# Four moved waits in a hybrid decoder layer: GLU weights, last transposes, Strassen operands, last GELU

## The reference

```
z = rmsnorm(h);  u,q,k,v,g,gate_a,gate_b = split(z @ W_in)
y = s5_scan(u) + D*u;  y = gelu(y);  y_a = y * sigmoid(y @ w_glu + b_glu)
y_b = retention(q,k,v) * silu(g)
h = h + (sigmoid(gate_a)*(y_a @ P_A) + sigmoid(gate_b)*(y_b @ P_B)) @ W_out
z = rmsnorm(h)
out = rmsnorm(h + relu(z @ W_up)^2 @ W_down)
```

## Time and profile before

| | |
|---|---|
| median of 3 runs | 1547.04 us (1545.83 to 1547.98) |
| the profiled execution | 1545.83 us, of which the span is 1544.0 us |
| granted TensorE clock | 0.995 of full speed over the span |
| busy share of the span | PE 98%, PE weight load 82%, DVE 61%, POOL 28%, ACT 20% |
| chain that ended last | PE 89%, DVE 7%, ACT 2% |
| one f32 matmul of 512 columns | starts 0.227 us after the one before it |

### The profile page before, as it was taken

The page is one execution under the profiler, slowest core; times in us unless marked ns, Lnnn a source line. Parts: engine busy times, 40 slices in busy tenths (PEclk is TensorE's granted clock), DMA queues, the critical chain, the costliest instruction groups (busy, mean ns, idle before and its releaser), DMA issues.

```text
span 1544.0 us, 21299 instructions
## 1 busy us (share of the span) xinstructions
PE 1509.7 (98%) x7474; PEld 1264.8 (82%) x7474; DVE 945.0 (61%) x1930; ACT 301.7 (20%) x585; POOL 431.7 (28%) x363
## 2 busy tenths in 40 slices
PE   5999999999999999999999999999999999999996
PEld 4888888889898988878888888888888888888885
DVE  7896856452565646475624788665555555555557
ACT  4211111300222222231101322111111111110114
POOL 5010100421010100103333004444444444444444
PEclk9999999999999999999999999999999999999998
DMA  7124534364110110113542010111111111111113
GB/s 227 69 95 109 137 107 110 109 222 146 28 56 27 43 39 27 45 38 123 177 170 69 1 44 11 55 55 54 54 54 54 54 54 52 43 54 54 47 42 130
DMA packets 98566, 119.20 MB, mean 77 GB/s; under 512 B 16296, under 2 KB 66640, under 8 KB 98512
## 3 DMA queue, kind: packets, MB, share of 16 engines
q1 hardware_dynamic: 67520, 78.22, 16.3%
q10 hardware_dynamic: 30992, 40.26, 8.2%
HBM read 96.56 MB, written 20.97 MB: 76 GB/s over the span
## 4 chain that ended last, share of the span: by engine, by line
PE 89%; DVE 7%; ACT 2%; ACTq 1%; issue 1%; DMA 0%; DVEq 0%; SPq 0%
PE acc L648 22%; PE acc L650 22%; PE acc L649 22%; PE aux L649 6%; PE aux L648 6%; PE aux L650 6%; PE aux L912 1%; PE aux L906 1%; PE aux L915 1%; DVE zb L2083 1%; ACT h_junk L1404 1%; DVE rs_tmp L1536 1%; PE aux L800 1%; PE aux L794 0%; PE aux L901 0%
## 5 line engine op out<-in xcount | busy, mean ns | idle before, releaser
L2154 DVE TENSOR_TENSOR h_res<-h_res,acc 128x512 f32<-128x512 f32 x240 | 159.9, 685 | 98.3 <-PE acc L650 97.0
L648 PE MATMUL acc<-dw_hi,hid_hi 128*128 128x512 f32 x512 | 199.4, 390 | 0.5 <-DVE h_res L2154 0.5
L650 PE MATMUL acc<-dw_hi,hid_lo 128*128 128x512 f32 x512 | 199.2, 389 | 0.0
L649 PE MATMUL acc<-dw_lo,hid_hi 128*128 128x512 f32 x512 | 199.2, 389 | 0.0
L648 PE MATMUL acc<-w_hi,z_hi 128*128 128x256 f32 (+1 forms) x512 | 189.0, 369 | 0.0
L521 POOL CAST w_hi<-stage 128x1024 fp32r<-128x1024 f32 x44 | 49.4, 1140 | 496.0 <-PE acc L650 333.1
L648 PE MATMUL acc<-z_hi,w_hi 128*128 128x512 f32 x448 | 177.9, 397 | 3.8 <-DVE z_lo L1516 3.8
L650 PE MATMUL acc<-z_hi,w_lo 128*128 128x512 f32 x448 | 175.4, 391 | 0.0
L649 PE MATMUL acc<-z_lo,w_hi 128*128 128x512 f32 x448 | 175.3, 391 | 0.0
L650 PE MATMUL acc<-w_hi,z_lo 128*128 128x256 f32 (+1 forms) x512 | 173.0, 338 | 0.0
L649 PE MATMUL acc<-w_lo,z_hi 128*128 128x256 f32 (+1 forms) x512 | 172.8, 338 | 0.0
(11 more groups left out here) (329 smaller groups left out, 2924.4 us busy)
## 6 DMA issues: line engine op xcount, KB each, us to landing
stage<-in_w_up SPq DMA_DIRECT2D x32, 512.0 KB, 4.0
stage<-in_w_down SPq DMA_DIRECT2D x32, 512.0 KB, 3.3
stage<-in_w_in SPq DMA_DIRECT2D x28, 512.0 KB, 4.0
gate_dram<-gate_t ACTq DMA_DIRECT2D x32, 256.0 KB, 2.1
x_in<-in_x SPq DMA_DIRECT2D x8, 512.0 KB, 7.6
stage<-in_w_in SPq DMA_DIRECT2D x32, 128.0 KB, 2.5
stage<-in_w_in SPq DMA_DIRECT2D x16, 256.0 KB, 3.3
gb_t<-gate_dram ACTq DMA_DIRECT2D x16, 256.0 KB, 3.0
```

Source lines behind the costliest of these rows:

```text
L648: nc.tensor.matmul(out, s_hi, m_hi_, start=first, stop=False)
L649: nc.tensor.matmul(out, s_hi, m_lo_, start=False, stop=False)
L650: return nc.tensor.matmul(out, s_lo, m_hi_, start=False, stop=last)
L2154: V.tensor_tensor(h_res[:, c, hs], h_res[:, c, hs], acc[:, p % 4, :], ALU.add)\
```

## The change

Four edits. (1) POOL no longer waits for `scanned` ahead of the GLU weights; its waits for `w_ready` and for tile 35 stay. (2) `turn_z2(6)` stays ahead of tile 161; `turn_z2(7)` moves from there to ahead of tile 162, just in front of PE's wait for the last `m_lo`. (3) In plain block 1 the eight subtractions of S2, S3, S1 and S4 follow every second down tile (after tiles 1, 3, 5, 7, 8, 10, 12 and 14 of 0 to 15), where six stood among the tiles and two behind the last; and PE waits once, for all eight, ahead of the first Strassen block, where it waited ahead of the second, third, fourth and sixth product for what these read. (4) In the last batch ACT's `gelu_sigmoid` comes behind gate tile 39 and its DMA, where it came ahead of them.

```diff
@@ gpsimd
             pool.wait_ge(w_ready, LD_GLU)
-            pool.wait_ge(scanned, MT)
             for i in range(2):
                 regular(LD_GLU + i, GR_GLU, i, (LD_GLU + i) // 2, OUT_GLU - 4)
@@ tensor, plain_block
-                        if f == 0 and n == OUT_MLP + 1:
-                            turn_z2(NCH - 2)
-                            turn_z2(NCH - 1)
+                        if f == 0 and n in (OUT_MLP + 1, OUT_MLP + 2):
+                            turn_z2(NCH - 3 + n - OUT_MLP)
                         if f == 0 and half == 1 and q == 0:
                             pe.wait_ge(lo_done, SP_Z2 + 16)
@@ tensor, win_block
-                if not first:
+                if first:
+                    pe.wait_ge(s_done, 8)
+                else:
                     pe.wait_ge(taken, g * 7)
...
                     pe.wait_ge(t_ready, g * 7 + (i + 1))
-                    if first and i in (1, 2, 3, 5):
-                        pe.wait_ge(s_done, 2 * (1, 2, 3, 0, 4)[i - 1])
@@ scalar, batch
                 for o in range(8):
-                    if o == 7 and steps is STEPS_LAST:
-                        gelu_sigmoid(b)
                     gate(o)
...
             batch(MT - 1, STEPS_LAST)
+            gelu_sigmoid(MT - 1)
             for i in range(2):
                 act.wait_ge(gate_sent[i], 64 * MT)
@@ vector, plain_block
-                    if f == 1 and (j, p) in ((0, 1), (0, 4)):
-                        lo_s(1 + p // 4, s2_hi, s2_lo, s2_sum, p // 4)
-                    if f == 1 and (j, p) in ((0, 7), (1, 1)):
-                        lo_s(3 + j, s3_hi, s3_lo, s3_sum, j)
-                    if f == 1 and j == 1 and p in (3, 5):
-                        lo_s1(p // 2 - 1)
-                if f == 1:
-                    for u in range(2):
-                        lo_s(7 + u, s4_hi, s4_lo, s4_sum, u)
+                    if f == 1 and j == 0 and p in (1, 3):
+                        lo_s(1 + p // 2, s2_hi, s2_lo, s2_sum, p // 2)
+                    if f == 1 and j == 0 and p in (5, 7):
+                        lo_s(1 + p // 2, s3_hi, s3_lo, s3_sum, p // 2 - 2)
+                    if f == 1 and j == 1 and p in (0, 2):
+                        lo_s1(p // 2)
+                    if f == 1 and j == 1 and p in (4, 6):
+                        lo_s(5 + p // 2, s4_hi, s4_lo, s4_sum, p // 2 - 2)
```

## The result

The changed kernel takes 1554.65 us (median of 5 runs, 1554.1 to 1555.4), against 1546.2 us for the kernel before in runs beside it: ratio 1.0053, 95% interval 1.0041 to 1.0064. The forecast was 1554.9 us, slower with chance 0.92. Over this and all later sessions the 27 executions of the changed kernel lie between 1550.07 and 1557.02 us; the profiled one took 1552.96. Two executions are left out of the comparisons in this document as slow: one of the kernel before (5583.11 us) and one of c2 (1690.08 us, granted clock 0.849).

The account below looks back on a forecast made before the run. PE, busy 98% of the span, bounds the kernel, so time changes only where PE idles. Edits 1, 4, 2, 3 cost 1.8 + 1.9 + 2.1 + 2.1 = 7.9 us; 1547.04 + 7.9 = 1554.9 us, range 1551.2 to 1557.2.

Parts of the forecast that it names:

- Turns, their order: Scan: DVE and POOL alternate, the waiting side next; cast before L1837, subtraction before L1838; PE loses 1.8 us.
- the two slowed operations: Scan: L1837 and L1838, 1.23 us each before, end at 268.1 and 271.6; L1838 over 3 us long.
- the free pass of the two operations with a PSUM operand: End of scan: two 0.68 us DVE operations reading PSUM are not held up by POOL's second cast.
- the other reading: Scan, without the skill's rule: the second cast holds up the PSUM operations as well, edit 1 costs 2.6 us.
- The branch that could have made it 0: Last GELU, rival: lo_y(3) goes ahead of POOL's second subtraction, edit 4 costs 0; margin 0.2 to 0.5 us; chance 0.12.
- DVE's lag sets the pace up to plain block 1: After tile 161: its subtraction comes 2.1 us later, and the whole DVE lag counts, not only 1.0 at tile 162.
- DVE's count of 15 adds, 8 subtractions and 1.25 us of hold-up: Plain block 1: DVE work up to the eighth subtraction, from 941.97 to 961.4, 2.1 us after 959.38 with the hop.
- No giving back: Behind 961 nothing returns the loss; rival: window loop gives it back, 1547 to 1548; given back or nothing, chance 0.06.
- The signs: Expected PE waits: 1.8 us for `hst`, 1.9 last `y_hl`, 1.9 `m_lo` at tile 162, 2.1 last `s_lo`.
- Its "seven" waits: Kernel before, whole span: PE waits seven times, the longest 11.5 us at the very start.
- The sum: Costs of edits 1, 4, 2 and 3: 1.8 + 1.9 + 2.1 + 2.1 = 7.9 us; all four costs, chance 0.62.
- The base of the forecast: Median time of the kernel before, 1547.04 us, to which the 7.9 us were added.

Follow-up runs that it names:

- c2: Kernel before plus early GLU cast (subtraction behind scan), last transposes inside tile 161, new subtraction order with four waits, late sigmoid with P_A work held until lo_y(3); 1545.3 us, ratio 0.9995.
- b4: Kernel before with edit 4 alone, plus POOL's first P_A cast held until lo_y(3) is done; stretch to chunk 5 597.00 us, 0.58 above before.
- a2: Kernel before with edit 2 alone; ratio 1.0018 [1.0008, 1.0028], stretch to plain block 1 49.35 us (47.13 before).
- a3: Kernel before with edit 3 alone, both halves; ratio 1.0016 [1.0007, 1.0026], stretch to Strassen 46.65 us (44.70 before).
- b3: Kernel before with edit 3's new DVE order of subtractions, keeping the four waits of before; stretch to Strassen 44.69 us (44.70 before).
- b5: Kernel before with edit 3's one wait for all eight subtractions, keeping DVE's order of before; PE wait 3.05 us, stretch to the end 586.3 us.

## Why the prediction was right, point by point

- **Edit 1**, 1.8 forecast, 1.69 measured. Turns, their order, the two slowed operations (1.97 and 3.31) and the free pass of the two operations with a PSUM operand (0.69 and 0.68 us, while the second cast ran, issued at 269.13 and over at 271.16) came as worked out. The Trainium skill (SBUF — State Buffer, section Who interferes with whom) says that a VectorE instruction with at most one SBUF input, outside the 2-port perf modes, does not contend with GpSimd. The two lengths agree with it; the sum by the other reading was 2.6.
- **Edit 4**, 1.9 forecast, 1.9 measured. The branch that could have made it 0 was decided by 0.8 us, not by the 0.2 to 0.5 I had. b4 shows that POOL's turns are the whole of it at that place. Whether that branch would have cost nothing is not shown: in b4, where `lo_y` runs first, POOL's work meets the next products and 0.45 us is lost.
- **Edit 2**, 2.1 forecast, 2.22 measured. The step "DVE's lag sets the pace up to plain block 1" is shown by a2 in DVE's rows and in the two new bank waits. So is the split: 0.9 to 1.0 us at tile 162, the rest in bank waits.
- **Edit 3**, 2.1 forecast, 1.95 to 1.97 measured. DVE's count of 15 adds, 8 subtractions and 1.25 us of hold-up was 0.05 us too long against a3 (subtraction eight from 959.99 to 961.21, where PE's bank wait shows that execution 0.1 ahead). b3 and b5 show that the wait costs and the order does not.
- **No giving back**: the stretch behind the first Strassen matmul is 584.6 before and 584.5 to 585.2 in the others (586.3 in b5); no kernel makes up there what it lost.
- **The signs**: the pauses of PE were 1.5 to 1.8 us, where the list of signs had 1.8 to 2.1. A cost counts starts of matmuls and a pause is shorter than that, since a row takes it from the end of the matmul before (0.39 us long, while the next could start 0.227 after it): 1.53 + 0.39 - 0.227 is the 1.69 of edit 1. The prediction used its costs for pauses. Its "seven" waits in the kernel before are seven rows of the list, with nine waits; nothing hangs on it.
- **The sum** was 7.9 and is 7.8. That the total of 1554.65 lies 0.25 from the forecast is partly luck. The base of the forecast was 1547.04, and the kernel before took 1546.2 beside the changed one, so the measured difference is 8.45: a base 0.84 too high and a difference 0.55 too small partly cancel. The stretches at both ends move by more than that from one execution to the next.

## What to carry to other kernels

On an engine that is busy 98% of the time, every moved wait is judged by the spare time behind it: list for each what must still run between the signal and the wait, on each engine in its own order, POOL's turns with DVE included. A wait that joins several ends with the latest of them, and the idle time seen at the wait is not the whole bill where the helper engine's lag sets the pace further on. To measure such parts, cut the span at operations common to both kernels; the whole time hides 2 us.

## What the runs showed of the hardware beyond that

- DVE operations with two SBUF operands and POOL operations went strictly by turns of whole instructions wherever they met in the places shown here: a 128 x 1024 cast held DVE for 0.74 us (1.97 against 1.23), a subtraction of that size for 2.1 (3.31 against 1.23 in the changed kernel).
- In b5, one execution, a PE pause of 3.05 us was followed by 3.4 us at the lower clock level (0.43 us a matmul, 1.2 GHz; 2.4 GHz before it); pauses of 1.5 to 1.8 us in the changed kernel were not. On top of the 3.2 us that the stretch to Strassen grew, this cost some 1.4.
- Executions of the same work differed by up to 3.6 us before tile 35 (262.54 to 266.15), where PE waits for the first loads and norms.
